# Moving two row fetches and one table load in the output stage of a gMLP, S5 and mixture-of-experts step

## What is computed

```
y = gelu(y.reshape(Bn, L, D_B))
b_out = y * sigmoid(y @ w_glu + b_glu)
mix = concatenate([a_out, b_out], axis=-1) @ w_out
x = x + gt1 * mix
h = rms_norm(x, g_norm2) * (1 + sc2) + sh2
x = x + gt2 * hier_moe(h, w_group, b_group, w_expert, b_expert, w1, w3, w2)
```

## Time and profile before

| | us |
|---|---|
| median of 3 runs | 1575.84 |
| lowest and highest of them | 1574.88, 1577.71 |
| the profiled execution, its own time | 1570.62 |
| its span from first to last instruction | 1568.9 |
| mean granted TensorE clock | 0.911 |
| PE busy in the span | 1294.7 (83%) |
| DVE busy | 941.4 (60%) |
| ACT busy | 589.3 (38%) |

### The profile page before, as it was taken

How to read it: one execution, slowest core, us unless ns; L and a number is a source line. 1 busy time by engine, 2 the same in 40 slices (tenths; PEclk the granted TensorE clock), 3 DMA queues, 4 the chain that set the end, 5 groups by cost and what they waited for, 6 DMA issues and landing times. The chain is left out here.

```text
span 1568.9 us, 25749 instructions
## 1 busy us (share of the span) xinstructions
PE 1294.7 (83%) x6758; PEld 1033.3 (66%) x6759; DVE 941.4 (60%) x2187; ACT 589.3 (38%) x981; POOL 470.9 (30%) x563
## 2 busy tenths in 40 slices
PE   4999999998969589879999268999999999998000
PEld 0777777876657477768887146777788787786000
DVE  2666655746368445445655775865454765763598
ACT  3652442413323231212221006865444775763121
POOL 1282131303224200000010004564422564553331
PEclk9999999998979889989999558999999999999555
DMA  9554535442568655455644046996675897883886
GB/s 348 147 161 133 194 104 186 145 135 77 180 228 296 166 185 166 150 163 165 204 142 134 14 180 249 383 382 253 256 261 205 304 425 289 307 320 134 334 324 258
DMA packets 119674, 340.67 MB, mean 217 GB/s; under 512 B 26749, under 2 KB 47449, under 8 KB 106146
## 3 DMA queue, kind: packets, MB, share of 16 engines
q1 hardware_dynamic: 87898, 250.40, 44.1%
q0 software_dynamic: 26656, 88.76, 17.1%
q10 hardware_dynamic: 5040, 0.52, 0.2%
HBM read 245.09 MB, written 96.50 MB: 218 GB/s over the span
## 5 line engine op out<-in xcount | busy, mean ns | idle before, releaser
L2409 POOL TENSOR_TENSOR down_lo<-expert_raw,down_hi (+1 forms) x64 | 153.2, 2415 | 201.1 <-ACT down_hi L2503 201.1
L2553 DVE TENSOR_TENSOR up_lo<-expert_raw,up_hi (+1 forms) x128 | 157.7, 1291 | 22.8 <-ACT up_hi L2498 21.4
L262 PE MATMUL ps_up<-up_hi,xT_hi 128*128 x400 | 162.3, 406 | 5.1 <-DVE up_lo L2553 2.9
L264 PE MATMUL ps_up<-up_hi,xT_lo 128*128 x400 | 157.1, 393 | 0.0
L263 PE MATMUL ps_up<-up_lo,xT_hi 128*128 x400 | 156.9, 392 | 0.0
L2498 ACT ACTIVATE up_hi<-expert_raw (+1 forms) x128 | 125.1, 1057 | 2.2 <-issue 1.1
L1761 POOL DMA_DIRECT2D expert_rows<-blank x31 | 26.7, 896 | 282.8 <-DVE x L1954 278.8
L1801 PE MATMUL ps_out<-wout_hi,catT 128*128 128x512 f32 (+1 forms) x272 | 109.3, 402 | 0.0
L1802 PE MATMUL ps_out<-wout_lo,catT 128*128 128x512 f32 (+1 forms) x272 | 107.1, 394 | 0.0
L1803 PE MATMUL ps_out<-wout_hi,catT 128*128 128x512 f32 (+1 forms) x272 | 107.1, 394 | 0.0
L262 PEld LDWEIGHTS ps_up<-up_hi,xT_hi 128*128 128x128 f32 x400 | 75.8, 190 | 24.1 <-issue 9.7
(11 more groups left out here) (434 smaller groups left out, 3146.6 us busy)
## 6 DMA issues: line engine op xcount, KB each, us to landing
expert_raw<-in_w SPq DMA_DIRECT2D x96, 1024.0 KB, 8.0
expert_rows<-yo SPq DMA_DIRECT2D x49, 512.0 KB
x<-in_x_prompt SPq DMA_DIRECT2D x32, 512.0 KB, 5.0
stage<-in_w_ada SPq DMA_DIRECT2D x32, 512.0 KB, 4.4
expert_rows<-blank POOLq DMA_DIRECT2D x31, 512.0 KB, 4.9
wada_early<-in_w_ada SPq DMA_DIRECT2D x8, 1024.0 KB, 18.5
s_tables<-pair_scratch POOLq DMA_DIRECT2D x32, 256.0 KB, 2.6
x_rows<-x SPq DMA_DIRECT2D x16, 512.0 KB, 2.7
```

Source lines behind the costliest of these rows:

```text
L262: pe.matmul(out, left(0, k), right(0, k), start=k == 0, stop=False)
L264: last = pe.matmul(out, left(1, k), right(0, k), start=False, stop=k == n - 1)
L2409: pool.tensor_tensor(down_piece(down_lo, run, m), raw_piece(run, 2, m, 1), down_piece(down_hi, run, m).bitcast(F32), ALU.subtract).then_in ...
L2553: dve.tensor_tensor(up_piece(up_lo, run, m), raw_piece(run, m // 2, m % 2, KD // 2), up_piece(up_hi, run, m).bitcast(F32), ALU.subtract).t ...
```

## The change

The rule for the place of `load_y` is replaced by a table `FETCH`: from place to group, with a flag that puts the fetch between the two stores of the place instead of ahead of both. Group 1 stays at the start of place 0 and group 4 at the start of place 9. Group 2 moves from the start of place 3 to place 2, behind the store of `x2`. Group 3 moves from the start of place 6 to place 5, behind the store of `x2`. The 24 loads of the sample's rows move from ahead of the loop to place 12 (`NT - 5`), ahead of its two stores.

```diff
+        FETCH = {0: (1, False), 2: (2, True), 5: (3, True), 9: (4, False)}
...
-                for n, c in enumerate((2, 4, 3)):
-                    for q in range(NSEQ):
-                        sp.dma_start(table_s[q * DSEQ:(q + 1) * DSEQ, n, :],
-                                     S.ada_d[1 + q:2 + q, c * D:(c + 1) * D].to_broadcast([DSEQ, D])).then_inc(mods_ld, 16)
                 for m, i in enumerate(TILES):
                     g = group_of(m)
-                    if g + 1 < NG and m == max(before[g + 1] - 4, before[g]):
-                        load_y(g + 1)
+                    if m in FETCH and not FETCH[m][1]:
+                        load_y(FETCH[m][0])
...
+                    if m == NT - 5:
+                        for n, c in enumerate((2, 4, 3)):
+                            for q in range(NSEQ):
+                                sp.dma_start(table_s[q * DSEQ:(q + 1) * DSEQ, n, :],
+                                             S.ada_d[1 + q:2 + q, c * D:(c + 1) * D].to_broadcast([DSEQ, D])).then_inc(mods_ld, 16)
                     sp.wait_ge(x2_ok, m + 1)
                     sp.dma_start(rows(S.x2_d, i), x2[0:rows_in(i), m % 4, :]).then_inc(x2_out[m % 4], 16)
+                    if m in FETCH and FETCH[m][1]:
+                        load_y(FETCH[m][0])
                     sp.wait_ge(h2_ok, m + 1)
```

## The result

The changed kernel takes 1565.1 us (median of 5 runs, 1561.95 to 1569.03) against 1575.84 us (5 runs, 1571.83 to 1579.38): a ratio of 0.9932, with a 95% interval of 0.9907 to 0.9958. It is faster by 10.7 us, and the interval leaves 6.6 to 14.7. The forecast was 1561.4, so the direction and the range held, and the gain came out at three quarters of the 14.45 us worked out.

What follows compares the result with a forecast made beforehand. PE was taken to bound the output stage, its waits for late-fetched rows on the path. Gains of 5.92 + 8.53 = 14.45 us off the median 1575.84 gave 1561.4 us, range 1558.5 to 1567.5.

Steps and rivals of the forecast that it cites:

- What bounds the kernel: Output stage: PE bounds it; its waits of 4.10 and 7.02 us ahead of groups 2 and 3 are on the path.
- Part 1: Group 2's fetch to place 2: PE's wait goes whole with 2.94 us to spare, clock stays full; 5.92 us gained.
- Part 2: Group 3's fetch to place 5: PE's wait goes with 0.41 us to spare; 8.53 us gained.
- the 0.50 us of waiting that I had counted: Group 3's glu: PE waits 0.50 us at the third slice until ACT's first sigmoid has read the first.
- The unseen cost: Traffic beside the moved fetches: landing 1.96 us, at most 2.94, issue unchanged; at 2.94 group 3's gain falls 0.98 to 7.55.
- The signs that I named: Changed profile: fetches 0.62 us each, group 3's y_high 12 us after the store, clock 1.00, stage 14 us shorter.
- three signs of being wrong: Fetches over 0.9 us each to issue, rows over 3 us after the last issue, or a new PE wait behind group 3.
- the main case: Both PE gaps close, 1558.5 to 1563.2 us with run spread and dearer landing; chance 0.74.
- The fetch lands late: Rival: moved fetches take 3 us more to land; gain 9.4 to 11.4, time 1564.4 to 1566.4 us; chance 0.15.
- SP's issue slows behind a full queue: Rival: 1.25 us per fetch issue and 2.94 to land give 1580.9 us, deciding from about 1.14 an issue; chance 0.03.
- Landing at high load: By the skill page's rule, each fetch lands 1.8 us later, group 3 loses 1.8 us, time about 1563.
- Parts 3 and 4: Delayed h2 stores (3.7 and about 1.3 us) cost nothing; sample's rows at place 12 cost 0, at worst 0.8 us.

Runs made afterwards that it cites:

- e1: The changed kernel measured once more, nothing altered; ratio 0.9928 to the kernel before.
- e2: The changed kernel with POOL's blanking DMAs spread so that none falls on places 2 and 5; ratio 0.9890 to the kernel before.
- e3: The changed kernel with four blanking DMAs instead of two at places 2 and 5, none at 1 and 4; ratio 0.9965 to the kernel before.
- e4: The changed kernel with the fetches of groups 2 and 3 ahead of the x2 store of places 2 and 5; ratio 0.9894 to the kernel before.
- f1: The changed kernel with the two blanking DMAs of places 2 and 5 issued by ACT instead of POOL; ratio 0.9938 to the kernel before.
- h1: The changed kernel with blanking from a wide source, 4 KB per partition instead of 512 bytes read eight times; ratio 0.9920 to the kernel before.
- f3: Of the change, only group 3's fetch and the sample's rows moved, group 2's fetch put back; ratio 0.9955 to the kernel before.
- h2: The changed kernel with the wide blanking source and SP issuing the blanking of places 2 and 5; one run, place 2 to 7 in 94.97 us.
- g1: The changed kernel with SP issuing the blanking of places 2 and 5 between x2 store and fetch; one run, place 2 to 7 in 97.45 us.

## Why the prediction was right, and where it was off

**What bounds the kernel: right.** PE's two gaps were time on the path. The stage shortened by what PE gained at the two groups, and from place 7 to place 16 it took 137.14 us before and 137.16 after. The barrier behind it passed everything on.

**Part 1, group 2: 5.92 us forecast, 4.94 measured** (648.28 - 619.83 = 28.45 us from the store of `x2` to the end of `glu`, now 647.80 - 624.29 = 23.51). The wait went whole and the clock stayed up. Two things were off. The fetch took 9.20 us to issue, not 7.53, and 2.49 to land, not 2.00, so that ACT's start moved by less; and for this group I named PE's own work as what is late next, with 2.94 us to spare, without asking when the third slice could start. ACT came 2.10 us late, and PE waited 0.81 us. The `glu` took 9.52 us instead of 8.38, and as PE came to it 0.16 us sooner than reckoned, 0.98 of the 5.92 was lost. So that chain (rows, `add_out`, square, sigmoid) had about 1.1 us to spare, not 2.94.

**Part 2, group 3: 8.53 us forecast, 5.73 measured** (711.43 - 677.32 = 34.11 us, now 705.21 - 676.83 = 28.38). The mechanism and the 0.41 us to spare were right; the failed term is the 9.87 us of issue, which came to 11.79. With 0.16 more to land and 0.05 less ahead of the issue, the rows came 2.03 us later than reckoned. Less the 0.41 this is the gap of 1.61. The clock that fell behind it made `glu` 705.21 - 692.61 = 12.60 us instead of 10.92, which cost 1.68, and that took the place of the 0.50 us of waiting that I had counted: 1.61 + 1.68 - 0.50 = 2.79, and 8.53 - 2.79 = 5.74. In e1, where the clock stayed up, the rows came 1.96 us late and the `glu` ended 703.32 - 675.60 = 27.72 us behind the store, 6.39 gained: there the late rows cost 2.14 us by themselves, because the third slice moves with them, as the prediction says. e2, where the issue is back at 0.62 us, gives the whole sum back. So the sum was right but for this price, and for the lower clock that one trace added to it.

**The unseen cost: the step that failed.** I bounded what the traffic beside the fetch does to its landing (1.96 to 2.94 us; measured 2.12 and 2.49, inside) and held the issue for fixed, "as the issue of 64 KB sets the pace". I had also let the bytes decide: 1.5 MB and 1.05 MB at 265 GB/s just fit into 9.87 us. On average they did fit: most issues took 575 ns even so. But while the DMA engines stood at 0.96, in the first microseconds, some issues were held to 1.33 and 1.53 us. Why they were held there and not at the same share in the kernel before stays open.

**The signs that I named.** The fetches started 0.4 us behind the store, and routing and experts lasted as long as before. The others failed: 0.77 and 0.74 us for each fetch instead of 0.62, ACT's `y_high` of group 3 14.3 us behind the store instead of 12, a gap of 1.61 us ahead of group 3, the lower clock behind it, and a stage shorter by 11.1 us instead of 14. None of the three signs of being wrong came (0.9 us an issue, 3 us to land, a new wait behind group 3). But the main case, both gaps closed, did not come true; the time fell into the range of the late landing.

**The rivals.** "The fetch lands late" is nearest to what happened, with 2.0 us instead of the 3 supposed, and by the issue rather than by the landing. "SP's issue slows behind a full queue" was the mechanism, though no run shows that a full queue does it, and I gave it 0.03 because I had priced only its extreme: 1.25 us an issue, where the runs show 0.75, and 1.01 with the blanking doubled. e3 shows that the rival was real: at 1.01 and 0.92 us the distance is 102.16 us, and of the gain 3.0 us are left. The 1.14 us an issue at which I let it decide is where group 2's rows come no earlier than before; for group 3 that point is 1.02, and the two together break even at 1.07. The evidence against it, that the fetches kept 0.62 us right behind a slow load, came from a place without the blanking.

**Landing at high load.** The landings came 0.49 and 0.16 us later than before (2.49 and 2.12 against 2.00 and 1.96), and in this change the load cost more by the issue, 1.67 and 1.92 us. By the Trainium skill's page "DMA: Bandwidth & Descriptors", section "Latency and other measured facts", an access to HBM takes 0.2 us on average and 2 us at high load, from which I estimated 1.8 us more. The change shows far less, but two other kernels come near it: 3.58 us in e4's group 3 and 642.46 - 638.72 = 3.74 us in e3's group 2, which is 1.6 and 1.7 us more. So the 2.94 us that I took for the upper bound wasn't one.

```profile
642.46 1.76 ACT L1863 ACTIVATE yT<-yf 128x384 fp32r<-128x384 f32 x4 [14.58 <-DMA yf<-s_out]
```

**Parts 3 and 4: right.** The stores of `h2` went out at 633.89 and 689.04, 3.0 and 5.6 us later behind their store of `x2` than before (1.3 and 3.7 forecast, with the shorter issue), and nobody waited for them. The 24 loads ended at 801.59 and held the store of `x2` until 801.63, 16.05 us behind the one of the place before instead of 15.49. That is 0.56 us late, within the 0.8 forecast, and the stage didn't notice.

## What to carry to other kernels

When a burst of small DMAs is moved next to large ones, price its issue as well as its landing: with 1 MB of stores more beside it, single issues were held here for up to 1.6 us, even though the bytes fitted on average. The busy share alone didn't foretell it. An event that releases several queues at once (here `x2_ok`: a store, two blanking DMAs and the fetch) is a bad place for a fetch that someone is waiting for; put it ahead of the event (e4), or spread the traffic that can wait (e2). And where a producer moves by x, list every consumer chain that hangs on it with its own slack: the shortest one decides, not the one that waits now.

## What the runs showed of the hardware

- A DMA of 64 KB in 512-byte rows costs SP 0.575 us to issue and 0.617 from one to the next. Beside 1.5 MB of other traffic single issues took up to 1.61 us (f1; 1.98 with 2.5 MB), and the mean 0.72 to 0.79, with the 1 MB in POOL's, ACT's or SP's own queue (0.69 to 0.74 from the wide source).
- 512 KB of zeros written by POOL from a source of 512 bytes read eight times landed after 4.7 to 5.6 us (median of each kernel, 5.0 in the change), from 4 KB rows after 4.5 and 4.6.
- From the last fetch's issue to ACT's start it took 1.7 to 2.5 us in most traces, but 3.58 us (e4) and 3.74 us (e3) with the blanking beside it.
- Of PE's gaps ahead of these two `glu`, those of 0.94 us (h1) and 1.55 us (e1) left the clock at its full level. Those of 1.59 (f3), 1.61 (the change and f1), 1.83 (h2), 2.90 (g1) and 3.31 us (e3), and all longer ones, brought the level of 1.2 GHz. The first matmul doesn't always show it. In e3 it took 0.41 us behind the gap of 3.31 us, as at full clock, but the granted clock was 0.50 soon after; behind the gap of 5.21 us the first one took 0.77 us already:

```profile
643.72 0.41 PE L1785 MATMUL ps_z<-yT,wglu_hi 128*128 128x384 f32 x1 [3.31 <-DVE yT L1926]
```

```profile
643.70:645.00 1.30, 1.28 (x5) 1.30 (x6) 1.30 (x4) 0.53 (x2) 0.00 (x0) 0.67 0.05 19
645.00:647.00 2.00, 2.00 (x7) 2.00 (x7) 1.97 (x3) 0.00 (x0) 0.00 (x0) 0.50 0.00 0
```

```profile
702.31 0.77 PE L1785 MATMUL ps_z<-yT,wglu_hi 128*128 128x512 f32 x1 [5.21 <-DVE yT L1926]
```
